# Hybrid encoder trunk: query norms in the exponent's scale, a spare stage tile, two residual tiles through DRAM, other ticks for the heads

## The reference

```python
def rms_norm(x, g):
    y = xf * lax.rsqrt(jnp.mean(xf * xf, axis=-1, keepdims=True) + EPS)
    return (y * g.astype(jnp.float32)).astype(x.dtype)

# layer 0                                     # layer 1
oa = neighbourhood_attention(rms_norm(qa, a_qn), rms_norm(ka, a_kn), va, a_rpb)
qb = axial_rope(rms_norm(qb, b_qn), rows, cols)
kb = axial_rope(rms_norm(kb, b_kn), rows, cols)
oc = window_gqa_sink(partial_rope(rms_norm(qc, c_qn), pos), partial_rope(rms_norm(kc, c_kn), pos), vc, c_sink)
od = dilated_attention(partial_rope(rms_norm(qd, d_qn), pos), partial_rope(rms_norm(kd, d_kn), pos), vd)
...
x = x + mixer(rms_norm(x, attn_norm[layer]), ...)
x = x + swiglu(rms_norm(x, ffn_norm[layer]), w_gate[layer], w_up[layer], w_down[layer])
```

## Time and profile before

| | us |
|---|---|
| median of three runs | 2155.07 (2153.96 to 2155.64) |
| the profiled execution | 2155.74 |
| its span, first to last instruction | 2153.9 |

### The profile page before, as it was taken

How to read it: one execution, slowest core, us unless ns; L and a number is a source line. 1 busy time by engine, 2 the same in 40 slices (tenths; PEclk the granted TensorE clock), 3 DMA queues, 4 the chain that set the end, 5 groups by cost and what they waited for, 6 DMA issues and landing times. The chain is left out here.

```text
span 2153.9 us, 27592 instructions
## 1 busy us (share of the span) xinstructions
PE 2123.2 (99%) x9424; PEld 1748.1 (81%) x9424; DVE 1399.0 (65%) x1853; ACT 997.1 (46%) x1253; POOL 79.4 (4%) x85
## 2 busy tenths in 40 slices
PE   8999999999999999999999999999999999999999
PEld 7778878888888888888887778778888888888887
DVE  6666678667666766566675666786677666765443
ACT  6455545444444444444454455454444444444443
POOL 0100001000000000000011010010000000000000
PEclk9999999999999999999999999999999999999999
DMA  8666646666666665555677564466666666656664
GB/s 272 202 184 191 215 147 203 195 183 191 204 194 185 186 204 187 185 190 194 210 217 230 169 200 144 135 195 199 193 184 193 202 192 185 192 188 205 214 203 139
DMA packets 218994, 414.59 MB, mean 192 GB/s; under 512 B 14512, under 2 KB 22960, under 8 KB 218928
## 3 DMA queue, kind: packets, MB, share of 16 engines
q1 hardware_dynamic: 216480, 409.51, 61.2%
q10 hardware_dynamic: 2448, 4.21, 0.6%
HBM read 403.97 MB, written 9.70 MB: 192 GB/s over the span
## 5 line engine op out<-in xcount | busy, mean ns | idle before, releaser
L857 DVE TENSOR_TENSOR w_lo<-w_raw,w_hi 128x1024 fp32r<-128x1024 f32 x760 | 907.6, 1201 | 630.1 <-ACT w_hi L602 624.2
L602 ACT ACTIVATE w_hi<-w_raw 128x1024 fp32r<-128x1024 f32 x760 | 785.5, 1040 | 946.4 <-PE psum L467 896.8
L464 PE MATMUL psum<-w_hi,xt_hi 128*128 128x512 f32 x2016 | 794.1, 394 | 8.1 <-DVE w_lo L857 5.0
L467 PE MATMUL psum<-w_hi,xt_lo 128*128 128x512 f32 x2016 | 786.0, 390 | 0.0
L465 PE MATMUL psum<-w_lo,xt_hi 128*128 128x512 f32 x2016 | 785.5, 390 | 0.0
L464 PEld LDWEIGHTS psum<-w_hi,xt_hi 128*128 128x128 f32 x2016 | 379.0, 188 | 90.5 <-DVE w_lo L857 10.3
L467 PEld LDWEIGHTS psum<-w_hi,xt_lo 128*128 128x128 f32 x2016 | 378.9, 188 | 79.8
L465 PEld LDWEIGHTS psum<-w_lo,xt_hi 128*128 128x128 f32 x2016 | 379.2, 188 | 78.0
L464 PE MATMUL psum<-w_hi,ht_hi 128*128 128x512 f32 x960 | 378.6, 394 | 6.0 <-DVE stage L890 2.9
L467 PE MATMUL psum<-w_hi,ht_lo 128*128 128x512 f32 x960 | 373.9, 389 | 0.0
L465 PE MATMUL psum<-w_lo,ht_hi 128*128 128x512 f32 x960 | 373.7, 389 | 0.0
(11 more groups left out here) (98 smaller groups left out, 644.7 us busy)
## 6 DMA issues: line engine op xcount, KB each, us to landing
w_raw<-in_w_gate SPq DMA_DIRECT2D x176, 512.0 KB, 3.7
w_raw<-in_w_up SPq DMA_DIRECT2D x176, 512.0 KB, 3.8
w_raw<-in_w_down SPq DMA_DIRECT2D x160, 512.0 KB, 4.0
w_raw<-in_cd_w_in SPq DMA_DIRECT2D x80, 512.0 KB, 4.0
w_raw<-in_ab_w_in SPq DMA_DIRECT2D x72, 512.0 KB, 4.0
w_raw<-in_ab_w_out SPq DMA_DIRECT2D x32, 512.0 KB, 3.6
w_raw<-in_cd_w_out SPq DMA_DIRECT2D x32, 512.0 KB, 3.6
w_raw<-in_w_down SPq DMA_DIRECT2D x32, 256.0 KB, 2.6
```

What stands on the lines that cost most here:

```text
L464: nc.tensor.matmul(acc, hi[:, chunk, ts], w_hi[:, slot, c, :], start=first and c == 0, stop=False)
L467: mm = nc.tensor.matmul(acc, lo[:, chunk, ts], w_hi[:, slot, c, :], start=False, stop=end)
L602: nc.scalar.activation(w_hi[:, slot, 0:n, :], w_raw[:, slot, 0:n, :], ACT.Copy).then_inc(hi_ready, 1)
L857: nc.vector.tensor_tensor(w_lo[:, slot, 0:n, :], w_raw[:, slot, 0:n, :], w_hi[:, slot, 0:n, :].bitcast(F32), ALU.subtract).then_inc(lo_rea ...
```

## The change

- Queries of A, B and C are not normalised any more. Their factor, rstd times the softmax scale, goes to `q_scale` (GpSimd, the same two instructions) and is the per-partition `scale` of the exponential; A's bias addition takes it as its scalar, now once per token half, and the negated maximum is multiplied by it (C: one more small DVE instruction for the sink). D's queries are scaled as before. C's and D's query gains beyond the rotated columns are multiplied into the key gains, once.
- Evacuations alternate between `stage[0]` and the new `stage[3]`. q_a: block transpose at b+1, reduces at b+2. q_c: rotation and transpose at b+1, reduces at b+2. q_d: rotation and reduces at b+1, scaling and transpose at b+2. q_b: reduces at b+1, rotation and transpose at b+2. k_c, k_d: transpose at b+3. The write to DRAM and the finishing copy go by the tick of the transpose (`block_tick`, +8 and +6).
- Residual tiles 0 and 1 of each output stage: one whole block transpose (behind the split of unit END+3) in place of 16 pieces, then the way over `block_dram` to `land_sb` (SP ahead of units END+8 and END+9). `residual_hi` at END+8, `residual_lo` at END+9, in halves by token.
- The heads' ticks are others, and small tensors lie in front of the large ones in SBUF.

```diff
-AB_ITEMS = ([("b", h, 25 + 2 * h, 30 + 2 * h, 32 + 2 * h) for h in range(8)]
-            + [("a", h, t, t + 4, t + 6) for h, t in enumerate((48, 50, 52, 54, 72, 73, 74, 75))])
-CD_ITEMS = ([("d", s, 41 + 4 * s, 46 + 4 * s, 82 + s) for s in range(4)]
-            + [("c", h, t, t + 4, t + (6 if h < 4 else 5)) for h, t in enumerate(
-                (65, 67, 69, 71, 73, 74, 75, 76, 81, 82, 83, 84))])
+AB_ITEMS = ([("b", h, 25 + 3 * h, 30 + 3 * h, 32 + 3 * h) for h in range(8)]
+            + [("a", h, t, t + 4, t + 6) for h, t in enumerate((50, 53, 56, 59, 72, 73, 74, 75))])
+CD_ITEMS = ([("d", s, 43 + 4 * s, 48 + 4 * s, pv) for s, pv in enumerate((82, 83, 84, 87))]
+            + [("c", h, t, t + 4, pv) for h, (t, pv) in enumerate(
+                ((63, 69), (65, 71), (67, 73), (69, 75), (71, 77), (73, 79), (74, 80), (75, 81),
+                 (79, 85), (81, 86), (82, 88), (83, 89)))])
...
+    def raw_stage(self, p):
+
+        return 3 * (self.qk_rank[p] % 2)
+
+    def block_tick(self, p):
+
+        kind = self.tiles[p][1]
+        return self.qk_tick(p, {"q_a": 1, "q_c": 1, "k_c": 3, "k_d": 3}.get(kind, 2))
...
-            def move_qk(layer, v):
+            def move_blocks(layer, v):
 
                 m = mixers[layer]
-                for q, p in enumerate(m.qk_tiles):
-                    _, kind, h0 = m.tiles[p]
+                moves = [(m.block_tick(p) + RING + LEAD + 1, p) for p in m.qk_tiles]
+                moves += [(KU * len(m.tiles) + OUT_END[n] + RING + LEAD + 1, None) for n in range(2)]
+                for i, (at, p) in enumerate(moves):
+                    move = m.move0 + i
+                    kind = "residual" if p is None else m.tiles[p][1]
                     run = TOK * 32 * (2 if kind == "kv_b" else 4)
-                    at = m.qk_tick(p, 2) + RING + LEAD + 1
                     if v == at:
-                        sp.wait_ge(qk_blocks, m.qk0 + q + 1)
-                        sp.dma_start(block_dram[:, :, 0:run], turn_sb[:, :, 0:run]).then_inc(blocks_out, 16)
+                        sp.wait_ge(blocks_ready, move + 1)
+                        if move:
+                            sp.wait_ge(landed, 64 * move)
+                        sp.dma_start(block_dram[:, :, 0:run], turn_sb[:, :, 0:run]
+                                     ).then_inc(blocks_out, 16)
                     if v == at + 1:
-                        sp.wait_ge(blocks_out, 16 * (m.qk0 + q + 1))
-                        if kind[0] == "q" and m.finish_rank[p]:
-                            sp.wait_ge(qk_ready, m.finish_rank[p])
-                        dst = land_sb[:] if kind[0] == "q" else keys_tensor(kind)[:, h0 // 4]
+                        sp.wait_ge(blocks_out, 16 * (move + 1))
+                        if kind[0] == "k":
+                            dst = keys_tensor(kind)[:, m.tiles[p][2] // 4]
+                        else:
+                            dst = land_sb[:]
+                            done = m.finish_rank[p] if p is not None else m.finished + len(m.finish_rank)
+                            if done:
+                                sp.wait_ge(qk_ready, done)
+                            if i == len(moves) - 1:
+                                sp.wait_ge(tile_split, split_count(layer, "out", 1))
                         dst = dst.rearrange("p a t c i -> p a (t c i)")
                         for b in range(4):
                             src = block_dram[:, b, 0:run].rearrange("(a j) x -> j a x", a=4)
-                            sp.dma_start(dst[32 * b:32 * b + 32], src).then_inc(qk_landed, 16)
+                            sp.dma_start(dst[32 * b:32 * b + 32], src).then_inc(landed, 64 // 4)
...
-                    act.wait_ge(qk_blocks, m.qk0 + m.qk_rank[p])
+                raw = stage[m.raw_stage(p)] if kind[0] in "qk" else None
+                if kind[0] in "qk" and m.qk_rank[p] > 1:
+                    act.wait_ge(blocks_ready, m.move0 + m.qk_rank[p] - 1)
...
-                    if t == m.qk_tick(p, 8 if kind[-1] != "a" else 7) and p in m.finish_rank:
-                        act.wait_ge(qk_landed, 64 * (m.qk0 + q + 1))
+                    if p in m.finish_rank and t == m.block_tick(p) + 6:
+                        act.wait_ge(landed, 64 * (m.move0 + q + 1))
...
-                                ins = nc.scalar.activation(probs[:, n % 3, tok, :], src, ACT.Exp, bias=bias, scale=SCALE,
-                                                           accum_out=den)
+                                ins = nc.scalar.activation(probs[:, n % 3, tok, :], src, ACT.Exp, bias=bias,
+                                                           scale=query_scale(m, kind, h)[:, tok:tok + 1], accum_out=den)
...
+            def residual_blocks(layer, n):
+
+                m = mixers[layer]
+                wait_residual(dve, layer, "out", n)
+                blocks(m.move0 + len(m.qk_tiles) + n, stage[0], 4)
...
+                    for c in range(2 * half, 2 * half + 2):
+                        hi = xt_hi[:, bass.ds(n * 4 + c, 1), :].rearrange("p c t -> p (c t)").bitcast(F32)
+                        lo = xt_lo[:, bass.ds(n * 4 + c, 1), :].rearrange("p c t -> p (c t)")
+                        parts = [(lo, turn_sb[:, c, :], hi)]
+                        if moved(name, n):
+                            hi, lo = (v.rearrange("p (t a i) -> p t a i", t=TOK, a=4) for v in (hi, lo))
+                            parts = [(lo[:, tok], landed_chunk(c)[:, tok], hi[:, tok]) for tok in range(TOK)]
+                        for part, src, high in parts:
+                            ins = nc.vector.scalar_tensor_tensor(out=part, in0=src,
+                                                                 scalar=gain_x[:, gain, bass.ds(n * 4 + c, 1)],
+                                                                 in1=high, op0=ALU.mult, op1=ALU.subtract)
...
+            def blocks(move, src, nh):
+
+                if move:
+                    dve.wait_ge(blocks_out, 16 * move)
...
+            def scale_heads(layer, q, dst, src):
+
+                nh = dst.shape[2]
+                for tok in range(TOK):
+                    dve.wait_ge(hrstd_ready, TOK * (mixers[layer].qk0 + q) + tok + 1)
+                    r = head_rstd[:, tok, 0:nh].unsqueeze(2).broadcast_to([P, nh, DH])
+                    ins = nc.vector.tensor_tensor(dst[:, tok], src[:, tok], r, ALU.mult)
+                step.then(ins)
+
+            def query_tile_work(layer, q, p, after):
+
+                m = mixers[layer]
+                kind = m.tiles[p][1]
+                raw, spare = stage[m.raw_stage(p)], stage[2]
+                rope = heads_of(raw, 4)[:, :, :, 0:32]
+                if after == 1:
+                    dve.wait_ge(acc_free[0], 2 * (ph["in", layer]["a"] + p + 1))
+                    if m.move0 + q:
+                        dve.wait_ge(blocks_ready, m.move0 + q)
+                    if kind in ("q_c", "q_d"):
+                        rotate_partial(0 if kind == "q_c" else 2, rope, heads_of(spare, 4)[:, :, :, 0:32],
+                                       heads_of(spare, 4)[:, :, :, 32:64], rope)
+                    if kind in ("q_a", "q_c"):
+                        blocks(m.move0 + q, raw, 4)
+                    else:
+                        head_squares(layer, q, 4)
+                if after == 2:
+                    if kind == "q_b":
+                        dve.wait_ge(hssq_ready, TOK * (m.qk0 + q + 1))
+                        rotate_axial(0, heads_of(spare, 4), heads_of(stage[1], 4), heads_of(raw, 4))
+                        blocks(m.move0 + q, spare, 4)
+                    elif kind == "q_d":
+                        scale_heads(layer, q, heads_of(raw, 4), heads_of(raw, 4))
+                        blocks(m.move0 + q, raw, 4)
+                    else:
+                        head_squares(layer, q, 4)
+
+            def key_tile_work(layer, q, p, after):
+
+                m = mixers[layer]
+                kind = m.tiles[p][1]
+                nh = 2 if kind == "kv_b" else 4
+                raw, spare = stage[m.raw_stage(p)], stage[2]
+                if after == 1:
+                    head_squares(layer, q, nh)
+                if after == 2:
+                    if m.move0 + q:
+                        dve.wait_ge(blocks_ready, m.move0 + q)
+                    scale_heads(layer, q, heads_of(spare, nh), heads_of(raw, nh))
+                    if kind == "kv_b":
+                        rotate_axial(1, heads_of(raw, nh), heads_of(stage[1], nh), heads_of(spare, nh))
+                        blocks(m.move0 + q, raw, nh)
+                    elif kind == "k_a":
+                        blocks(m.move0 + q, spare, nh)
+                    else:
+                        which = 1 if kind == "k_c" else 3
+                        flat0, flat2 = (t[:].rearrange("p t (h d) -> p (t h) d", d=DH) for t in (raw, spare))
+                        g = cd_gain_sb[:, which, 32:DH].unsqueeze(1).broadcast_to([P, 8, DH - 32])
```

(37 more changed lines are left out.)

173 lines of the change are left out of this document (81 added, 92 removed).

## The result

The changed kernel took 2132.66 us (median of 4 runs, 2131.87 to 2134.09) beside 2155.36 of the kernel before: 0.9895 of its time, 95% interval 0.9878 to 0.9912. That is 22.7 us less; 2130.2 us was forecast. The profiled execution took 2131.87, 23.9 less than that of before, with a span of 2130.1.

The account below looks back on a forecast made before the run. TensorE was taken to lose 32.7 us in the mixer stages to late DVE and ACT work. Gains of 8.2, 9.1, 3.8 and 3.8 sum to 24.9, from the median 2155.07 to 2130.2 us; range 2126 to 2141.

Parts of the forecast that it names:

- The bound: Four mixer stretches: TensorE loses 32.7 us together, about 2.0 at the start, so at most some 30 us can be won.
- Input stages: Input projections of both layers: gains of 8.2 us in layer 0 and 9.1 in layer 1 from waits, restarts and clock.
- the returns it named: Layer 1's input stage: about 0.5 us each comes back at ticks 30 and 38, 0.4 at tick 46.
- The finishing copies: Ticks 63, 71, 79 of layer 1: 0.3 us to spare; tick 72 of layer 0: about 0.5 late.
- half of it: Rival: copies late by 5.5 us, ticks 30, 38, 46 of layer 1 lose 5.5; 11 less, 2141; chance 0.17.
- Output stages: Output projections of both layers: 3.8 us gained in each as w_lo waits, small slips and late residual adds go.
- `xt_lo` in halves: Output stages: residual_lo as 16 halves in place of 8 wholes costs at most 3.8 us more, half of that nearer.
- 2.7 to the write's landing: Residual moves on SP: first term of a 7.6 us move, before 1.75 to issue reads and 3.6 until landing.
- I take zero: Residual moves, output stages: no cost to TensorE, bounds 0 and 7.6 us each.
- three units of ring cover the rest: Output stages: load 20 leaves about 2 us after its slot frees; the ring's three units cover what remains.
- The slower rival: SP's queue at output units 20 and 24: moves reach TensorE's path, 30.4 us against 24.9 gained, 2160.6; chance 0.04.
- Exponent's scale: Exponential on ACT: per-head scale is another operand of the same instruction, at nothing; were it dearer, ACT is half idle.

Follow-up runs that it names:

- dead: Changed kernel with two dead products added on DVE at the second tick of each q_a, q_b and q_c tile: 2137.97 us.
- Q: Label of the part on query and key tiles (lighter, shared between ticks); its query tiles alone on the kernel before: 2146.45 us.
- I: Label of the part with the heads' new ticks; those of A, B and D alone on the kernel before: 2153.95 us.
- noR: Changed kernel with residual tiles 0 and 1 turned in 16 pieces on DVE again, no way over DRAM: 2138.89 us.
- deadlate: Changed kernel with two dead products per q_a, q_b and q_c tile at the fourth tick instead of the second: 2135.35 us.
- best: Changed kernel with q_d reducing first, query and key reads back one unit later, and residual tile 1's `xt_lo` two ticks later: 2135.03 us.
- none: Changed kernel with query and key work, heads' ticks and residual tiles all taken back, keeping SBUF layout and two stage tiles: 2156.61 us.
- noI: Changed kernel with the old ticks of all heads: 2139.20 us.
- onlyQ: Kernel before's work with the change's query tiles alone, old heads' ticks, residual tiles in 16 pieces: 2146.45 us.
- onlyI: Kernel before's work with the new ticks of A, B and D heads alone, C's old ones: 2153.95 us.
- slow1: Changed kernel with each residual tile read back one extra time, waited for, before the reads that count: 2152.59 us.

## Why the prediction was right, and where its reasons were not

**The bound** of some 30 us was the right frame: the feed-forward stages did not move, and after the change 8.9 of the 32.7 us are left, 2.0 of them (an estimate) the start.

**Input stages.** Forecast 8.2 and 9.1, measured 7.6 and 9.2. That the scalings mattered is shown by dead, which gives back the 1.3 us per tile and no wait and returns 4.6 us of the two stages' loss. The prediction listed Q's and I's waits as separate gains; the losses above show that I's exists almost only with Q's. The sum did not suffer, since both were made. Of the returns it named, tick 38 of layer 1 lost 1.1 instead of 0.5, with q_d's scaling and its 0.90 for GpSimd before the transpose as said, and nothing was lost at ticks 30 and 46. The finishing copies at ticks 63, 71, 79 and 72, named with 0.3 us of room, made no wait; the room held, and the rival "half of it" fell with them.

**Output stages.** Forecast 3.8 each, measured 3.2 and 3.9. That the 16 pieces were what made units 20 and 24 late is shown by noR. `xt_lo` in halves: eight start 0.265 apart and take 2.2 us a tile against 1.7 in four wholes, so 0.5 a tile or 1.0 a stage. That is a quarter of the bound of 3.8, where half was called nearer.

**The residual moves: right number, and a term that was too short.** The term that was mis-sized is "2.7 to the write's landing", and with it "7.6 us" for a move. From the issue of the write to the last landing the four moves took 10.4, 10.3, 10.3 and 10.1 us, and their writes 3.9, 5.7, 4.3 and 5.9. The 2.7 was the median of 14 writes of the input stages; these four stood behind weight loads. "I take zero" held nearly (0.3 us at unit 24 in layer 0, nothing in layer 1), and so did "Were a landing 2 us longer, ACT would wait 1, out of the ring's reserve, and TensorE nothing": ACT waited 1.1 to 1.5 before each `xt_hi`. But that took the whole reserve, and that it sufficed is luck, for the longer moves weren't in the sum.

The step that failed with it reads "three units of ring cover the rest". Load 24 landed 9.2 us after its slot was free in layer 0 (298.47 to 307.66) and TensorE waited 0.3; 8.8 us in layer 1, and it waited not at all. In deadlate it was 10.0 with a wait of 1.5, in dead 10.3 with 1.6. In best, with `xt_lo` out of the way on DVE, it was 10.5 without a wait, so the point depends on what DVE has to do there. The slower rival had named the place and the point, "the ring's three units (8 us)"; for load 24 it lay near 9, and the kernel after stands on it (load 20 landed 9.3 after its slot was free and cost nothing). Its price of a move's length was right in size: 4 x 4.9 = 19.6 more gave 19.9 more of time, the clock's part in it, and 39.2 more gave 36.0. So 0.04 was too little for it. By that slope each move 1 us longer than measured would cost up to 4 us in all, an estimate.

The diff also has a wait on `tile_split` ahead of tile 1's reads, which I did not cost. It lasts 4.1 us but ends 0.1 and 0.4 us before the write lands, so in the kernel after it added nothing. In deadlate it ended last, by 0.7.

The Trainium skill's rule weighed there (page "DMA: Bandwidth & Descriptors", section on the anatomy of one DMA) gives a move 6.4 us and would have made it even if all of it lay on the path. The median write's 2.9 us agrees with its 3.2; the four residual writes, behind loads in the queue, took up to 5.9, and the moves over 10. Where the rule speaks against the change it is right by the measured slope, and what saved the change is that the move's length still fitted, not that it was cheap.

**Exponent's scale.** Forecast "at nothing". The instruction went from 473 ns (none has 474 with the constant, the group below) to 559 with the per-partition operand, 3.5 us over 40 of them, all of it on ACT, which has the time in these stages. The Trainium skill has this price (page "ScalarE: Activation LUTs", section on what ACT_TABLE_LOAD costs: each pointer operand adds about 93 ns), and the rows agree with 86. It changed no number here, but I should have counted it ahead of the copies with 0.3 us of room. In none:

```profile
L788 ACT ACTIVATE probs<-psum,negmax 128x256 f32<-128x256 f32 x40 | 18.6, 474 | 22.4 <-DVE negmax L1162 12.4 <-DVE negmax L1159 10.0
```

**The clock** term of 1.7 us was there in the kernel before and is gone after (1.00 in every stage). Tying it to the one long stall was less sure than I wrote, see below.

## What to carry to other kernels

Before a transfer is taken as hidden behind a ring, follow every wait in front of its issue, also the one for the tile it lands in, and count what is queued ahead of it in the DMA engines: a write that took 2.7 us in a quiet stage took up to 5.9 behind weight loads. Two moves in one queue run in a row, and a delay of the first is added to the second. Where two waits end together, look at which ended last before one is blamed. An order written by hand has its gains tied to each other: the new ticks were worth some 2 us with the old query tiles and 7 with the light ones, and moving 2 us of DVE work out of one unit's way (best) put the same stall at the next add. The cheapest test of a reserve is to lengthen the thing itself by a known amount and read at which instruction the time comes out.

## What the runs showed of the hardware

The same stall did and did not lower TensorE's clock. In noI and in onlyQ TensorE stood 3.12 us for the same probabilities at tick 58 of layer 1. In noI the matmuls after it stay at 0.39, in onlyQ they go to 0.63 within 1.4 us. The granted clock of the 10 us after it is 1.00 in noI, and 0.57 over 1240 to 1244 in onlyQ, where it was at 1.2 GHz for 3.4 us (PE of noI, then of onlyQ):

```profile
1236.83 0.66 PE L509 MATMUL psum<-ident_sb,probs 128*128 128x128 f32 x4 [3.12 <-DVE probs L1177]
...
1238.47 0.39 PE L492 MATMUL psum<-w_hi,xt_lo 128*128 128x512 f32 x1
```

```profile
1239.08 0.66 PE L513 MATMUL psum<-ident_sb,probs 128*128 128x128 f32 x4 [3.12 <-DVE probs L1182]
...
1240.45 0.63 PE L493 MATMUL psum<-w_hi,xt_hi 128*128 128x512 f32 x1
```

In other runs the clock fell after idle times of 1.8 us (none after 1244.7, onlyI after 100.3), and stayed up after one of 3.0 (none at 110.7). What decides was not settled; a fall cost 1.7 us here and up to 2.6 (slow1), so single stalls of 1.8 to 3.3 us carry that uncertainty beside their own length.

A write of 512 KB from SBUF to DRAM landed 2.6 to 2.9 us after its issue in the kernel before, in every case, and 3.9 to 7.1 us in the output stages of after and slow1, where weight loads had been issued just ahead of it (three in a row for the 7.1).
